# Identity products in TensorE's waits at five stage borders, and row stores moved from the latent stage into attention

## The reference

```python
mod = silu(c) @ ada_w[layer] + ada_b[layer]        # 6 rows of 1024: shift, scale, gate, twice; one set for c, one for c_ctx
h = rmsnorm(x, norm1_g) * (1 + scale) + shift       # both streams
layer 0: y = [latent attention(h), RG-LRU(h)] @ w_out
layer 1: y = [windowed attention(h), SSD(h)] @ w_out    # latents only
x = x + gate * y
x = x + gate2 * moe(modulate(x, norm2_g, shift2, scale2))   # 32 experts, top 2, weights 6 MB an expert
```

## Time and profile before

| | us |
|---|---|
| median of three runs | 1572.16 |
| the profiled execution | 1580.67 |
| its span, first to last instruction | 1578.8 |
| TensorE (products) busy | 1266.2 (80%) |
| TensorE weight loads busy | 725.5 (46%) |
| DVE busy | 601.2 (38%) |
| ACT busy | 391.7 (25%) |
| mean granted TensorE clock | 0.902 of full |

### The profile page before, as it was taken

One profiled execution on the slowest core, in us unless ns is written; L12 is line 12 of the kernel. 1 busy time (PEld: TensorE's weight loads), 2 busy tenths in 40 slices (PEclk: granted clock), 3 DMA queues, 4 the chain that ended last, 5 costly groups with the idle time before them and its releaser, 6 DMA issues. The chain is left out here.

```text
span 1578.8 us, 36656 instructions
## 1 busy us (share of the span) xinstructions
PE 1266.2 (80%) x14918; PEld 725.5 (46%) x14919; DVE 601.2 (38%) x1633; ACT 391.7 (25%) x821; POOL 32.9 (2%) x76
## 2 busy tenths in 40 slices
PE   4998979985899997778753799879798997666766
PEld 3445646553565554434421546644354553333333
DVE  2456665327222221112212556765633333122212
ACT  2173333213222222212212322543211111101101
POOL 0102020000000000000001000000000000000000
PEclk9999999997999998989977799969799999888888
DMA  9602988449899999999997520063899999999997
GB/s 359 236 31 99 329 300 315 166 169 383 352 405 427 428 431 429 428 430 429 428 428 302 186 76 1 1 257 139 349 384 425 420 428 429 428 429 428 428 429 320
DMA packets 82715, 507.65 MB, mean 322 GB/s; under 512 B 12965, under 2 KB 17378, under 8 KB 56018
## 3 DMA queue, kind: packets, MB, share of 16 engines
q1 hardware_dynamic: 76152, 489.21, 75.6%
q10 hardware_dynamic: 3306, 8.78, 1.5%
q0 software_dynamic: 3184, 8.63, 1.4%
HBM read 494.58 MB, written 12.01 MB: 321 GB/s over the span
## 5 line engine op out<-in xcount | busy, mean ns | idle before, releaser
L1703 PE MATMUL bank<-sb_ring,sb_scratch 128*32 128x256 f32 x2240 | 141.2, 408 | 50.2 <-DMA sb_ring<-in_moe_w_up 41.2
L1924 PE MATMUL bank<-sb_ring,sb_scratch 128*32 128x256 f32 x1664 | 120.2, 452 | 63.7 <-DMA sb_ring<-in_moe_w_up 58.9
L1789 DVE TENSOR_TENSOR sb_scratch<-sb_scratch,bank 128x128 f32<-128x128 f32 x50 | 14.4, 288 | 317.3 <-ACT sb_scratch L1742 317.3
L1703 PEld LDWEIGHTS bank<-sb_ring,sb_scratch 128*32 128x32 f32 x2240 | 78.3, 118 | 110.9 <-DMA sb_ring<-in_moe_w_up 39.2
L1924 PEld LDWEIGHTS bank<-sb_ring,sb_scratch 128*32 128x32 f32 x1664 | 61.9, 129 | 120.8 <-DMA sb_ring<-in_moe_w_up 59.4
L1746 ACT ACTIVATE sb_scratch<-bank 32x256 f32<-32x256 f32 x200 | 74.9, 374 | 162.8 <-PE bank L1718 161.0
L2009 DVE TENSOR_TENSOR sb_scratch<-sb_scratch,bank 128x128 f32<-128x128 f32 x38 | 10.9, 287 | 242.4 <-ACT sb_scratch L1965 242.4
L1674 PE MATMUL bank<-sb_h,sb_scratch 128*32 128x256 f32 x1632 | 99.4, 384 | 3.7 <-DVE sb_scratch L1776 3.3
L1965 ACT ACTIVATE sb_scratch<-bank 128x128 f32<-128x128 f32 x38 | 10.5, 277 | 366.3 <-PE bank L1924 366.3
L1703 PE MATMUL bank<-sb_scratch 128*32 128x256 f32 x960 | 60.1, 407 | 22.8 <-DMA sb_scratch<-in_moe_w_up 20.1
L1148 PE MATMUL bank<-sb_ring,sb_scratch 128*128 128x512 f32 x160 | 74.2, 616 | 4.7 <-DVE sb_x L1155 3.6
(11 more groups left out here) (410 smaller groups left out, 1880.5 us busy)
## 6 DMA issues: line engine op xcount, KB each, us to landing
sb_ring<-in_moe_w_gate SPq DMA_DIRECT2D x40, 2048.0 KB, 26.5
sb_ring<-in_moe_w_up SPq DMA_DIRECT2D x40, 2048.0 KB, 31.4
sb_ring<-in_moe_w_down SPq DMA_DIRECT2D x39, 2048.0 KB, 33.2
sb_ring<-in_ada_w SPq DMA_DIRECT2D x21, 2048.0 KB, 13.5
sb_scratch<-in_moe_w_gate SPq DMA_DIRECT2D x20, 2048.0 KB, 27.3
sb_scratch<-in_moe_w_up SPq DMA_DIRECT2D x20, 2048.0 KB, 30.3
sb_scratch<-in_moe_w_down SPq DMA_DIRECT2D x20, 2048.0 KB, 31.9
sb_ring<-in_moe_w_gate SPq DMA_DIRECT2D x8, 1024.0 KB, 10.5
```

Source lines behind the costliest of these rows:

```text
L1703: last = nc.tensor.matmul(c.bank(1, 2, FQ)[MB * q:MB * q + MB, :, :], m.xt[:, k, :], m.gu[j][:, :, k, q * FQ:(q + 1) * FQ], start=k == 0, ...
L1789: v.tensor_tensor(m.hm, m.sg, c.ps[1][:, FQ:2 * FQ], ALU.mult).then_inc(hm_ready, 1)
L1924: last = nc.tensor.matmul(c.bank(1, 2, FQ)[MB * q:MB * q + MB, :, :], m.xt[:, k, :], m.gu[j][:, :, k, q * FQ:(q + 1) * FQ], start=k == 0, ...
```

## The change

The class that holds the buffers gets a helper that issues n products of the identity with the identity, repeated along the moving side. It is called at five places. In `first_stage` nine of 256 columns are written to an unused half of bank 1. In `mla_stage` six of 512 columns follow the turns of tile 1. In `combine_norm_stage` each stream's turns are preceded by a wait and by twelve or eight. In `project_ssd_stage` ten follow the last product. The eight stores of the latent stage's modulation rows and the wait for the last finished row leave SP's list there; `mla_stage` returns a function that issues the stores and waits for them, and `attention_stage` calls it at the head of SP's list, where it waited before.

```diff
+    def hold_clock(self, out, n):
+
+        width = out.shape[1] // P
+        for _ in range(n):
+            self.nc.tensor.matmul(out.rearrange("p (a f) -> p a f", f=P), self.ident[:],
+                                  self.ident[:].unsqueeze(1).to_broadcast([P, width, P]), start=True, stop=True, skip_group_check=True)
...
             turn_rows(2)
+            c.hold_clock(c.ps[1][:, 2 * P:4 * P], 9)
             product_of(3)
...
-            sp.wait_ge(ada_done, md.n)
-            md.store(sp, stored)
...
                 last.then_inc(query_turned, 1)
+                if t == 1:
+                    c.hold_clock(c.ps[0][:], 6)
...
-    return stored, 16 * md.Q * len(md.segments)
+
+    def store_rows(sp):
+        md.store(sp, stored)
+        sp.wait_ge(stored, 16 * md.Q * len(md.segments))
+    return store_rows
...
-            if rows_stored:
-                sp.wait_ge(*rows_stored)
+            if store_rows:
+                store_rows(sp)
...
             for s in streams:
+                pe.wait_ge(added, 1 if s == 0 else LT)
+                c.hold_clock(c.ps[0][:], (12, 8)[s])
                 for b in range(4):
...
             last.then_inc(y_mean, 1)
+            c.hold_clock(c.ps[0][:], 10)
```

More of the change, by code:

```diff
@@ L916, in _, with attention_stage @@
                     md.finish(a, 2 + a % 2, ada_done)
-    return stored, 16 * md.Q * len(md.segments)
-def attention_stage(c, units, qt, kt, v_of, scale, dst_t, p, pt, width, sink=None, mask=None, sp_work=None, sp_end=None, md=None, out=None, rows_stored=None, ada_in=None):
+    def store_rows(sp):
+        md.store(sp, stored)
+        sp.wait_ge(stored, 16 * md.Q * len(md.segments))
+    return store_rows
+def attention_stage(c, units, qt, kt, v_of, scale, dst_t, p, pt, width, sink=None, mask=None, sp_work=None, sp_end=None, md=None, out=None, store_rows=None, ada_in=None):
     nc = c.nc
@@ L2640, in program @@
         last_in = [c.sem(f"last_ada_w_in{j}") for j in range(3)]
-        rows_stored = mla_stage(c, m, late, used, [lambda sp, a=a: last.load_weights(sp, a, last_in[a]) for a in range(3)])
+        store_rows = mla_stage(c, m, late, used, [lambda sp, a=a: last.load_weights(sp, a, last_in[a]) for a in range(3)])
         wo_in = c.sem("ab_wo_in")
@@ L2650, in program @@
         attention_stage(c, units, m.qt, lambda h: m.kt[:, h, :], lambda h, k: m.v[:, k, h * VD:(h + 1) * VD],
-                        QK ** -0.5, m.attn_t, m.p, m.pt, QK, sp_work=loads, sp_end=lambda sp: load_expert(c, mo, sp, 0, 0), md=last, out=out, rows_stored=rows_stored, ada_in=last_in)
+                        QK ** -0.5, m.attn_t, m.p, m.pt, QK, sp_work=loads, sp_end=lambda sp: load_expert(c, mo, sp, 0, 0), md=last, out=out, store_rows=store_rows, ada_in=last_in)
         def first_weights(sp):
```

## The result

The change makes the kernel slower: 1578.94 us in the median of 13 executions (1574.59 to 1585.44), against 1573.49 (1567.99 to 1581.24) for 13 executions of the kernel before. The ratio is 1.0032, 95% interval 1.0017 to 1.0048, so about +5.0 us (2.7 to 7.6). Forecast were 1570.4 us and a range of 1562 to 1576.5.

A forecast was written before the change was run, and what follows sets the result against it. Taken as bound: the experts' weight stream late in each layer, which moves with every border shift at full worth. Terms 0, -1.0, -3.8, -0.9, +1.9 and +2.0 sum to -1.8 us: from 1572.16 to 1570.4 us, range 1562 to 1576.5.

The forecast's parts named there:

- The price of a hold: Length of the added products at full clock: two passes each; nine 3.9 us, six 5.1, twelve 10.3, eight 6.9, ten 8.6.
- First stage, "I take 0": Nine holds before the fourth chunk's product: 1.35 us late, a faster product pays back; 0, bounds -0.3 and +1.4 us.
- Latent stage, -1.0: Six holds before the up projection: it begins later but its first half runs at full clock; -1.0 us, bounds +1.85 and -2.1.
- Stores, -3.8 and -0.9: Border before attention: without store issues it is ACT's, -3.8 us; shorter idle keeps the clock up for first scores, -0.9.
- Combine, +1.9: Twelve and eight holds: second projection starts 3.6 us later, runs 1.7 faster; net +1.9 us, bounds +0.5 and +3.8.
- the projection's slow start: Second projection after the combine: 3.4 us of its work ran at half clock; holds would save 1.7 us.
- SSD's end, +2.0: Ten holds delay the border 4.0 us, faster attention scores give back 2.0; net +2.0 us, bounds -2.0 and +4.0.
- the overrun rival: Combine and SSD borders wait for the last hold, clock falls before useful products profit: +5.4 us, 1577.6 us; chance 0.13.
- Holds half as long: Rival, all five sites: one pass each or twice the speed, holds just fit their waits; -10.5 us, 1561.7 us; chance 0.17.
- The clock kept up through attention: Rival: holds pay back their overrun, SSD term -2.0, first attention saves 1.9; -6 in all, 1566 us; chance 0.14.
- No clock held: Rival: identity products hold no clock, all run at half speed after the combine wait; some +25 us, 1597; chance 0.03.
- the stores staying on the path: Rival, latent-to-attention border: another engine ends as late or SP is late; 3.8 us gain gone, +2 us, 1574.2; chance 0.03.

The follow-up runs named there:

- f2: The change without the ten SSD-end holds, stores moved: 1576.87 us, ratio 1.0008 to the kernel before.
- e4: The change without the combine and SSD holds; first-stage nine, latent six and moved stores stay: 1567.94 us, ratio 0.9968 to the kernel before.
- g1: The kernel before plus only the nine first-stage holds, stores not moved: 1574.09 us, ratio 1.0006 to the kernel before.
- e2: The change with all its holds but the stores back in the latent stage: 1582.35 us, ratio 1.0047 to the kernel before.
- e1: The change without any holds, only the stores moved: 1571.28 us, ratio 0.9977 to the kernel before.
- g2: The kernel before plus only the combine's twelve and eight holds with their wait, stores not moved: 1577.09 us, ratio 1.0025 to the kernel before.
- g3: The kernel before plus only the ten SSD-end holds, stores not moved: 1578.27 us, ratio 1.0023 to the kernel before.
- f4: The change without the first-stage and latent-stage holds, stores moved: 1579.35 us, ratio 1.0023 to the kernel before.
- f1: The change without the combine's twelve and eight holds, stores moved: 1579.02 us, ratio 1.0014 to the kernel before.
- f3: The change with no first-stage holds and 3, (6, 4) and 5 at the later sites, stores moved: 1563.96 us, ratio 0.9918 to the kernel before.
- e3: The change with 4, 3, (6, 4) and 5 holds for 9, 6, (12, 8) and 10, stores moved: 1566.63 us, ratio 0.9951 to the kernel before.
- g4: The change with no first-stage holds and 2, (3, 2) and 3 at the later sites, stores moved: 1565.44 us, ratio 0.9947 to the kernel before.

## Why the prediction was wrong

**The price of a hold** was right: 0.43 to 0.44 us a pass, 4.05, 5.32, 11.99, 7.03 and 8.75 us where 3.9, 5.1, 12.3, 6.9 and 8.6 were worked out. The Trainium skill's 216 ns for a 512-column product (TensorE: Matmul & The Clock Gate, Back-to-back issue gap) is half of what one of the two float32 passes took, so for this type it is no price, as the earlier trace rows said.

**First stage, "I take 0": failed.** The step read the wait's length, 2.55 us, from one execution. Its start moves by up to 3.3 us (holds from 29.62 in f2 to 32.61 in after and 32.94 in e4), with the clock over the products and turns ahead of it, and its end, the landing of the fourth chunk, doesn't move with it. In an execution like the one that was read, the 0 holds (41.03 in f2 against 41.20 in before); in the others the delay is 2.6 to 4.3 us. The traces give +2.5 us on average, the timing of g1 +1.0 (-1.6 to +3.5). The upper bound of +1.4 was too low, since it took the same start.

**Latent stage, -1.0: right.** -1.6 us with the stores moved (four traces against two), -0.9 with the stores as before (e2 against four), about -1 by the timed sums. The up projection took 7.98 us instead of 9.77, as forecast, in all kernels with holds there; but it did so in e1 and g1 as well, two of the six without.

**Stores, -3.8 and -0.9: right in mechanism, a bit too large by the clock.** The latent stage shrank by 4.5 us (81.3 on average in before, g1, g2 and g3, 76.8 in e1 and f4), the timing gives -3.6 (-7.1 to -0.2). The border is now ACT's, as read. With the stores moved, the eight score passes took 5.37 us in after, f1, f2 and f4, 6.85 in e1, and 3.67 in e4 and with the short holds; with the stores as before they took 6.3 to 6.7. So the clock's share came in some executions and not in others.

**Combine, +1.9: failed**, and this is a term where the range's bound held (+3.8) but the value didn't. The border was priced at +3.6 and measured at +4.0. The -1.7 for "the projection's slow start" failed: it was subtracted in full, though only three of the six traces without these holds show the loss. And over the whole second stage nothing is seen of it: from the second projection to the last SSD product the kernels without holds need 145.9 us on average (142.6 to 148.1) and those with (12, 8) 146.0 (144.3 to 147.2). Of the six, the three with a slow start took 147.9 and the three with a fast one 143.8: the stage is longer in the executions that start it slow, but the holds, which make the start fast every time, don't bring it to 143.8. Why is open. The timing of g2 is +3.9.

The sentence of the Trainium skill that I weighed there (same page, Part 4: PE-mode transpose), that transposes don't count as TensorE being busy the way products do, doesn't hold here: in e1 the granted clock was 0.50 over the 16 turns of stream 0 and 1.00 right after them, and went from 0.50 to 1.00 once more after the 16 turns of stream 1, with nothing but turns by the identity on TensorE before either rise; f1 and g1 show the same fast start. By it I had feared a fall over the last turns of after; there the clock is 1.00.

**SSD's end, +2.0: right by the traces** (+3.8 and -1.6, net +2.2, where +4.0 and -2.0 were forecast), and by timing +3.6 (0.3 to 7.1), which allows both it and the whole delay. That stays open.

**The sum.** By the timed parts: +1.0, about -1, -3.6, +3.9, +3.6 make +3.9, and after measured +5.0. The stretches of the traces give less, 2.5 - 1.6 - 4.5 + 4.0 + 2.2 = +2.6, just under the interval's 2.7. The forecast's -1.8 missed by two terms above all, the first stage (1.0 to 2.5 us) and the combine (2.0), and, by the timed parts, by 1.1 at the stores and 1.6 at the SSD. About 1 us of the +5.0 is in none of them. The case that came true is the overrun rival, +5.4, to which I gave 0.13. Its statement, that the border waits for the last hold, fits both late sites. Its reason for the missing gain, that the clock falls before useful products profit, doesn't fit the combine: the second projection started at full clock in all five kernels with (12, 8). There the gain is missing because the kernel without holds often starts fast too. So that its +5.4 is so near is in part luck. The range was too narrow on that side because all my clock gains came from one profiled execution, 8.5 us above the median, and the slow spells in it were priced as if every execution had them.

**The other rivals.** Holds half as long: refuted by the records, but halving their number gave about what it forecast at the combine (-1.4 where it said -1.7), at the SSD's end between -1.8 (f3) and -0.5 (e3), and its sum of -10.5 us is near f3's -13 and e3's -8. The clock kept up through attention: refuted, 0.74 over its first 20 us. Its sum was also wrong: from -1.8, a last term of -2.0 and a first attention of -1.9 give -6.8, 1565.4 us, not -6. No clock held, and the stores staying on the path: both refuted.

## What to carry to other kernels

A product that fills a wait must end before the wait does: until then it is free, and from there each microsecond is delay, while the clock it kept gave back less than half of it at the two late sites here. Size such fillers by the shortest wait over several executions, with a microsecond to spare; here a quarter of the number did nearly the same good, and the ones at full length turned 8 to 13 us of gain, 3.6 of it the stores', into 5 us of loss. And take the price of a slow clock from several traces of equal code before crediting anyone with removing it, because some executions never paid it.

## What the runs showed of the hardware that was not expected

- The same instructions with the same waits met the clock differently from execution to execution: the second modulation product took 1.95 us in seven traces and 3.25 to 3.64 in the other seven, the stage of the second projection and the SSD 142.6 to 148.1 us. With medians of a dozen executions the intervals are still 0.1 to 0.2% to either side.
- After a combine stage at half clock, with nothing but turns by the identity on TensorE, the clock was up at the projection's first pass in three of six kernels (e1, f1, g1); in e1 and g1 the record shows it up already between the two groups of turns, and down again during the second.
- Fewer holds did as much for the turns: in g4 the second stream's turns took 2.39 us, as in f3 with twice the products (1.93 in after). What makes the clock rise was not measured by itself.
- Eight store issues took SP 5.25 to 5.76 us at the end of the latent stage (before, g1, g2, g3, e2), but 3.35 (e1) to 4.61 us (f3) at the head of attention, for the same transfers. The cause was not looked for.
